# Three small transposes of the gate rows moved behind the first third of the fifth projection tile, in a one-core decoder step

## The chip, the cores and the metric

The kernel runs on one core of a Trainium2 chip. Its time is device time in microseconds (us); lower is better. TensorE (PE in the profile) multiplies, VectorE (DVE) and ScalarE (ACT) do the elementwise work, GpSimd (POOL) copies small histories, and SyncE (SP) issues the loads.

## What is computed

Two decoder layers are run on one batch of 336 tokens (256 of a prompt, 64 of eight sampled sequences, 16 meta tokens). Each layer is a half-step SwiGLU FFN, a token mixer, and a second half-step SwiGLU FFN. The part of the mixer that matters here, cut from the reference:

```
proj = h @ w_in
qkv, z = proj[..., OFF_Q:OFF_Z], proj[..., OFF_Z:OFF_BETA]
b_raw = proj[..., OFF_BETA:OFF_A]            # 4 gate columns
a_raw = proj[..., OFF_A:OFF_B]               # 4 gate columns
qkv = silu(causal_dw_conv(qkv_ext, conv_gdn))
q = l2_normalize(q of qkv) * GDN_DK ** -0.5;  k = l2_normalize(k of qkv)
beta = sigmoid(b_raw)
g = -exp(a_log) * softplus(a_raw + dt_bias)
o, s = gdn_chunks(q, k, v, beta, g, s0, chunk)
```

## The kernel before

All data is held features first: 128 features on the partitions, tokens along the row. Every float32 product of the weights is made of three passes of TensorE (L1493 to L1495, high by high, weights high by input low, weights low by input high), so each weight chunk is first split: ScalarE writes the high half (L734) and VectorE the low half (L1040). Weights come in chunks through three buffers.

The mixer's order of work is written out by hand as one list of steps, and each engine walks the same list and does its own share of each step (a step that has no share on an engine costs it nothing). So a place in the list is a place in the queue of all engines at once. The list begins with `HEAD`, and then come the parts: the projection of 28 tiles of 128 columns is cut in thirds of 3, 3 and 2 blocks of 128 features, so 9, 9 and 6 matmuls; `BEHIND_PART` says what stands behind each third. The first four tiles are made in the step `entry`, so `BEHIND_PART` begins with the first third of tile 4, the fifth tile.

The names that the prediction uses:
- `gate_rows`: TensorE multiplies the 8 gate columns (high and low) with the input, with the norm's own column sums (L1518) and row transposes (L1511, three transposes of 128x128) between.
- `gate_read`: VectorE scales the rows by the norm into ACCX (L1251).
- `gate_cols`: TensorE turns the rows into columns (L1726, three transposes); VectorE copies and adds them (L1254, L1255), adds the bias (L1259) and forms T1 (L1260), which raises `to_act`; ScalarE waits for that, then runs two exponentials (L896, L897), changes its function table, runs the logarithm (L898), and changes the table again to Silu (L899).
- `evac n`: VectorE reads projected tile n out of TensorE's output memory (L1198, L1200, L1201). `tap n`: ScalarE makes the first tap of its convolution (L838). `conv n`: VectorE makes the other three taps (L1180, three instructions). `silu n`: ScalarE (L856 to L858). `sq n`: ScalarE squares a q or k tile into SQX (L890). `sq_sum n`: TensorE sums the squares over the features (L1705).
- `gate_g`: VectorE finishes the gates (L1266 to L1273). `gb t`: TensorE spreads a column (L1662), VectorE forms the decay (L1294).
- The step `sq_sum n` waits on TensorE for `sq n`: `pe.wait_ge(qk_sq.sem, qk_sq.at(t, layer))`.

Of the kernel before, what the change touches and what calls it, by code (L numbers as in the profile page):

```python
# [105 lines left out]
def chunk_length(c):  # L106
# [3 lines left out]

FIRST_TILE = 4
HEAD = [
    ("entry",), ("gate_rows",), ("hi", 1, 0), ("evac", 0), ("tap", 0), ("hi", 1, 1), ("gate_read",), ("lo", 1, 0), ("gate_cols",),
    ("evac", 1), ("conv", 0),
]


BEHIND_PART = [
    [],
    [("evac", 2), ("evac", 3)],  # L120
    [],
    [("silu", 0), ("tap", 1), ("sq", 0), ("evac", 4), ("hi", 2, 0)],
# [1906 lines left out]
```

## Time and profile before

| | |
|---|---|
| time, median of 3 runs | 1414.47 us (1412.2 to 1415.42) |
| span of the profiled execution | 1412.4 us |
| TensorE busy | 1391.3 us, 99% of the span |
| VectorE busy | 862.0 us, 61% |
| ScalarE busy | 629.7 us, 45% |

The span runs from the first to the last instruction of one profiled execution. A time of its own outside the span is not given for that execution; the three timed runs are others. In rows of a timeline, the first number is the start and the second the time until the group's end, both in us; matmuls overlap, so the spacing of their starts (0.15 us for a matmul of 336 tokens) is what each adds.

### The profile page before, as it was taken

What the parts mean: (1) busy time and instruction counts of PE and PEld (TensorE: products, weight loads), DVE (VectorE), ACT (ScalarE), POOL (GpSimd) and SP (SyncE); (2) the same over time, 40 slices, a digit from 0 to 9 for tenths busy, and PEclk for the clock granted to TensorE, in tenths of its full rate; (3) what the DMA queues carried; (4) which work ended last, traced back from release to release, by engine and by line L of the source; (5) the groups of instructions that cost most, each with busy time, mean ns of one, the idle gap of its engine ahead of it and who ended that gap; (6) DMA issues with size and microseconds to landing.
All of it is one profiled execution on the core that took longest, in us unless ns stands there. A gap on an engine that the chain in (4) does not pass through costs nothing.

```text
span 1412.4 us, 25251 instructions
## 1 busy us (share of the span) xinstructions
PE 1391.3 (99%) x10788; PEld 1369.1 (97%) x10788; DVE 862.0 (61%) x1510; ACT 629.7 (45%) x1002; POOL 32.4 (2%) x130
## 2 busy tenths in 40 slices
PE   9999999999999999999999999999999999999997
PEld 8999999898999999999999999998999999999997
DVE  5655533787697765553376555337886968655433
ACT  5443333582644544433354333335826345444331
POOL 0000000110000000000000000001100000000000
PEclk9999999999999999999999999999999999999998
DMA  6544344422216334434435443444221263444342
GB/s 220 208 149 149 121 143 141 132 90 87 71 61 217 118 130 142 149 122 144 155 121 207 150 149 117 140 142 140 90 93 65 90 214 122 150 149 149 123 144 99
DMA packets 49760, 190.93 MB, mean 135 GB/s; under 512 B 6160, under 2 KB 8720, under 8 KB 49136
## 3 DMA queue, kind: packets, MB, share of 16 engines
q1 hardware_dynamic: 49040, 184.19, 38.9%
q0 software_dynamic: 608, 5.12, 0.9%
q8 instruction: 85, 1.39, 0.4%
q14 instruction: 27, 0.22, 0.0%
HBM read 182.86 MB, written 6.43 MB: 134 GB/s over the span
## 4 chain that ended last, share of the span: by engine, by line
PE 95%; DVE 3%; ACT 1%; issue 0%; DMA 0%; SPq 0%
PE PS L1493 27%; PE PS L1494 27%; PE PS L1495 27%; PE PS L1533 2%; PE PS L1664 2%; PE PS L1538 2%; PE PS L1534 2%; DVE WL L1040 1%; PE PS L1813 1%; PE PS L1662 1%; PE PS L1705 1%; ACT XH L751 1%; DVE XL L1052 1%; PE PS L1769 1%; PE PS L1788 1%; DVE X L1104 0%
## 5 line engine op out<-in xcount | busy, mean ns | idle before, releaser
L1493 PE MATMUL PS<-XH,WH 128*128 128x336 f32 (+1 forms) x1728 | 550.6, 319 | 0.0
L1495 PE MATMUL PS<-XH,WL 128*128 128x336 f32 (+1 forms) x1728 | 543.2, 314 | 0.0
L1494 PE MATMUL PS<-XL,WH 128*128 128x336 f32 (+1 forms) x1728 | 542.8, 314 | 0.0
L1040 DVE TENSOR_TENSOR WL<-RAW,WH 128x1024 fp32r<-128x1024 f32 (+1 forms) x312 | 398.8, 1302 | 193.3 <-ACT WH L734 192.8
L734 ACT ACTIVATE WH<-RAW 128x1024 fp32r<-128x1024 f32 (+1 forms) x312 | 343.1, 1118 | 222.0 <-DMA RAW<-in_w_down 173.3
L1493 PEld LDWEIGHTS PS<-XH,WH 128*128 128x128 f32 x1728 | 325.4, 188 | 1.4 <-issue 0.4
L1494 PEld LDWEIGHTS PS<-XL,WH 128*128 128x128 f32 x1728 | 325.5, 188 | 0.3
L1495 PEld LDWEIGHTS PS<-XH,WL 128*128 128x128 f32 x1728 | 325.2, 188 | 0.0
L1493 PE MATMUL PS<-HH,WH 128*128 128x336 f32 (+1 forms) x704 | 221.4, 314 | 0.0
L1494 PE MATMUL PS<-HL,WH 128*128 128x336 f32 (+1 forms) x704 | 221.3, 314 | 0.0
L1495 PE MATMUL PS<-HH,WL 128*128 128x336 f32 (+1 forms) x704 | 221.2, 314 | 0.0
L1146 DVE TENSOR_TENSOR GR<-PS,RB 128x336 f32<-128x336 f32 (+1 forms) x88 | 44.3, 503 | 186.5 <-PE PS L1495 186.4
L809 ACT ACTIVATE HH<-HF 128x336 fp32r<-128x336 f32 (+1 forms) x88 | 42.4, 482 | 204.3 <-DVE HF L1154 204.3
L1493 PEld LDWEIGHTS PS<-HH,WH 128*128 128x128 f32 x704 | 132.6, 188 | 0.0
L1494 PEld LDWEIGHTS PS<-HL,WH 128*128 128x128 f32 x704 | 132.2, 188 | 0.0
L1495 PEld LDWEIGHTS PS<-HH,WL 128*128 128x128 f32 x704 | 132.1, 188 | 0.0
L807 ACT ACTIVATE SG<-GR 128x336 f32<-128x336 f32 (+1 forms) x88 | 42.3, 480 | 117.8 <-DVE GR L1146 117.8
L1156 DVE TENSOR_TENSOR HL<-HF,HH 128x336 fp32r<-128x336 f32 (+1 forms) x88 | 44.4, 504 | 48.3 <-ACT HH L809 48.3
L1533 PE MATMUL PS<-XH,WH 128*128 128x336 f32 (+1 forms) x192 | 62.4, 329 | 4.6 <-DVE WL L1040 2.4
L1534 PE MATMUL PS<-XH,WL 128*128 128x336 f32 (+1 forms) x192 | 59.6, 314 | 0.0
L1538 PE MATMUL PS<-XL,WH 128*128 128x336 f32 (+1 forms) x192 | 47.6, 315 | 0.0
L1533 PEld LDWEIGHTS PS<-XH,WH 128*128 128x128 f32 x192 | 36.0, 187 | 10.7 <-DVE WL L1040 4.7
(252 smaller groups left out, 1220.7 us busy)
## 6 DMA issues: line engine op xcount, KB each, us to landing
RAW<-in_w_up SPq DMA_DIRECT2D x176, 512.0 KB, 4.3
RAW<-in_w_down SPq DMA_DIRECT2D x64, 704.0 KB, 4.1
RAW<-in_w_in SPq DMA_DIRECT2D x56, 512.0 KB, 4.3
RAW<-in_w_out SPq DMA_DIRECT2D x16, 512.0 KB, 4.2
SEQ_S<-in_states SPq DMA_DIRECT2D x2, 2048.0 KB, 9.7
out_state_s<-SEQ_S POOLq DMA_DIRECT2D x2, 2048.0 KB, 8.9
X<-in_x SPq DMA_DIRECT2D x8, 168.0 KB, 4.8
out_y<-X SPq DMA_DIRECT2D x4, 320.0 KB, 2.3
```

The source lines that it names most:

```text
L734: act.activation(WH[slot][:, cols], RAW[slot][:, cols], ACT.Copy).then_inc(split_hi.sem, 1)
L807: act.activation(SG[k][:, 0:n], GR[k][:, 0:n], ACT.Silu).then_inc(silu_done.sem, 1)
L809: act.activation(hidden(HH, c, n), HF[k][:, 0:n], ACT.Copy).then_inc(h_hi.sem, 1)
L1040: dve.tensor_tensor(WL[slot][:, cols], RAW[slot][:, cols], WH[slot][:, cols].bitcast(F32), ALU.subtract).then_inc(split_lo.sem, 1)
L1146: dve.tensor_tensor(GR[k][:, 0:n], PS[:, up_bank(c, 0), 0:n], RB[:, 0:n], ALU.mult).then_inc(gate_scaled.sem, 1)
L1156: dve.tensor_tensor(hidden(HL, c, n), HF[k][:, 0:n], hidden(HH, c, n).bitcast(F32), ALU.subtract).then_inc(h_lo.sem, 1)
L1493: pe.matmul(out, wh, xh, start=first, stop=False)
L1494: pe.matmul(out, wh, xl, start=False, stop=False)
L1495: return pe.matmul(out, wl, xh, start=False, stop=last)
L1533: pe.matmul(out, wh, XH[:, kt, 0:n], start=(kt == 0), stop=False)
L1534: pe.matmul(out, wl, XH[:, kt, 0:n], start=False, stop=False)
L1538: ins = pe.matmul(out, wh, XL[:, kt, 0:n], start=False, stop=(kt == KT - 1))
```

## The change

The step `gate_cols` leaves `HEAD`, where it stood behind `lo 1 0` and ahead of `evac 1` and `conv 0`, and stands behind the first third of tile 4.

```diff
 HEAD = [
-    ("entry",), ("gate_rows",), ("hi", 1, 0), ("evac", 0), ("tap", 0), ("hi", 1, 1), ("gate_read",), ("lo", 1, 0), ("gate_cols",),
-    ("evac", 1), ("conv", 0),
+    ("entry",), ("gate_rows",), ("hi", 1, 0), ("evac", 0), ("tap", 0), ("hi", 1, 1), ("gate_read",), ("lo", 1, 0), ("evac", 1),
+    ("conv", 0),
 ]
 BEHIND_PART = [
-    [],
+    [("gate_cols",)],
     [("evac", 2), ("evac", 3)],
```

On TensorE, at the end of `gate_rows` in the first layer, the three transposes stand ahead of tile 4 before. PS is the output memory, XH and XL the input's halves, WH and WL the weights' halves.

```order
L1714 MATMUL PS<-XH,W8X 16x336
L1726 MATMUL PS<-MK,ACCX 128x16 [waits evac_dve]
L1726 MATMUL PS<-MK,ACCX 128x16 x2
L1493 MATMUL PS<-XH,WH_59 128x336 [waits split_lo]
L1494 MATMUL PS<-XL,WH_59 128x336
L1495 MATMUL PS<-XH,WL_56 128x336
```

With the change, nine matmuls of tile 4 come first:

```order
L1714 MATMUL PS<-XH,W8X 16x336
L1493 MATMUL PS<-XH,WH_59 128x336 [waits split_lo]
L1494 MATMUL PS<-XL,WH_59 128x336
L1495 MATMUL PS<-XH,WL_56 128x336
L1493 MATMUL PS<-XH,WH_59 128x336
L1494 MATMUL PS<-XL,WH_59 128x336
L1495 MATMUL PS<-XH,WL_56 128x336
L1493 MATMUL PS<-XH,WH_59 128x336
L1494 MATMUL PS<-XL,WH_59 128x336
L1495 MATMUL PS<-XH,WL_56 128x336
L1726 MATMUL PS<-MK,ACCX 128x16 [waits evac_dve]
L1726 MATMUL PS<-MK,ACCX 128x16 x2
```

The transposes moved down by nine matmuls; nothing else moved on TensorE.

On VectorE at the same place, the four small instructions of the gate columns stand ahead of the reading of tile 1 and the convolution of tile 0 before (B_90 is the gate columns, EXT the projected tiles, CV_131 a convolution's buffer):

```order
L1251 TENSOR_TENSOR ACCX<-PS,RB 16x336 [waits filled]
L1040 TENSOR_TENSOR WL_57<-RAW_54,WH_60 128x1024 [waits split_hi]
L1254 COPY B_90<-PS 128x24 [waits small]
L1255 TENSOR_TENSOR B_90<-B_90,PS 128x24 [waits chain_dve]
L1259 TENSOR_TENSOR TOK<-B_90,GATE_P 128x12 [waits in_gate,chain_dve]
L1260 SCALAR_TENSOR_TENSOR TOK<-TOK 128x12 [waits chain_dve]
L1198 TENSOR_TENSOR EXT<-PS,RB 128x16 [waits hist_set,products]
L1200 TENSOR_TENSOR EXT<-PS,RB 128x256
L1201 TENSOR_TENSOR EXT<-PS,RB 128x8x8
L1180 SCALAR_TENSOR_TENSOR CV_131<-EXT,PAR_ALL,CV_131 128x360 [waits tap0]
L1180 SCALAR_TENSOR_TENSOR CV_131<-EXT,PAR_ALL,CV_131 128x360 [waits chain_dve] x2
```

With the change they stand behind both:

```order
L1040 TENSOR_TENSOR WL_57<-RAW_54,WH_60 128x1024 [waits split_hi]
L1198 TENSOR_TENSOR EXT<-PS,RB 128x16 [waits hist_set,products]
L1200 TENSOR_TENSOR EXT<-PS,RB 128x256
L1201 TENSOR_TENSOR EXT<-PS,RB 128x8x8
L1180 SCALAR_TENSOR_TENSOR CV_131<-EXT,PAR_ALL,CV_131 128x360 [waits tap0]
L1180 SCALAR_TENSOR_TENSOR CV_131<-EXT,PAR_ALL,CV_131 128x360 [waits chain_dve] x2
L1254 COPY B_90<-PS 128x24 [waits small]
L1255 TENSOR_TENSOR B_90<-B_90,PS 128x24 [waits chain_dve]
L1259 TENSOR_TENSOR TOK<-B_90,GATE_P 128x12 [waits in_gate,chain_dve]
L1260 SCALAR_TENSOR_TENSOR TOK<-TOK 128x12 [waits chain_dve]
L1198 TENSOR_TENSOR EXT<-PS,RB 128x16 [waits hist_set,products]
```

The four instructions passed six others. The same stands in the second layer. ScalarE's, GpSimd's and SyncE's queues keep their order.

## Rows read from the trace of the kernel before

**Rows 1.** The page: TensorE's busy time; the chain that ended last, by engine

```profile
PE 1391.3 (99%) x10788; PEld 1369.1 (97%) x10788; DVE 862.0 (61%) x1510; ACT 629.7 (45%) x1002; POOL 32.4 (2%) x130
...
PE 95%; DVE 3%; ACT 1%; issue 0%; DMA 0%; SPq 0%
```

**Rows 2.** Timeline of TensorE, first layer: start, time, engine, line, tiles, [idle before]

```profile
277.87 0.31 PE L1714 MATMUL PS<-XH,W8X 128*16 128x336 f32 x1
278.94 0.35 PE L1726 MATMUL PS<-MK,ACCX 16*128 16x16 f32 x3 [0.76 <-DVE ACCX L1251]
...
279.49 0.32 PE L1494 MATMUL PS<-XL,WH 128*128 128x336 f32 x1
```

**Rows 3.** Timeline of TensorE: three transposes in flow, between matmuls

```profile
276.63 0.31 PE L1717 MATMUL PS<-XL,W8X 128*8 128x336 f32 x1
276.78 0.49 PE L1511 MATMUL PS<-MK,RC 128*128 128x128 f32 x3
...
277.26 0.31 PE L1717 MATMUL PS<-XL,W8X 128*8 128x336 f32 x1
```

**Rows 4.** Timeline of VectorE, first layer

```profile
278.40 0.48 DVE L1251 TENSOR_TENSOR ACCX<-PS,RB 16x336 f32<-16x336 f32 x1
...
279.95 0.16 DVE L1254 COPY B<-PS 128x24 f32<-128x24 f32 x1
...
280.66 0.17 DVE L1198 TENSOR_TENSOR EXT<-PS,RB 128x16 f32<-128x16 f32 x1
...
282.96 0.17 DVE L1198 TENSOR_TENSOR EXT<-PS,RB 128x16 f32<-128x16 f32 x1
...
285.12 1.85 DVE L1180 SCALAR_TENSOR_TENSOR CV<-EXT,PAR_ALL,CV 128x360 f32<-128x360 f32 x3 [0.44 <-ACT CV L838]
```

**Rows 5.** Timeline of ScalarE, first layer: gate columns, a tap, squares

```profile
280.77 0.21 ACT L896 ACTIVATE TOK<-B 128x12 f32<-128x12 f32 x1 [0.61 <-DVE TOK L1260]
...
284.50 0.58 ACT L838 ACTIVATE CV<-EXT,PAR_ALL 128x360 f32<-128x360 f32 x1
284.99 0.51 ACT L890 ACTIVATE SQX<-QKV 128x384 f32<-128x384 f32 x1
...
288.07 0.51 ACT L890 ACTIVATE SQX<-QKV 128x384 f32<-128x384 f32 x1
...
291.59 0.51 ACT L890 ACTIVATE SQX<-QKV 128x384 f32<-128x384 f32 x1
...
312.39 0.92 ACT L890 ACTIVATE SQX<-QKV 128x384 f32<-128x384 f32 x2
```

**Rows 6.** Timeline of TensorE, first layer: the sums of squares

```profile
288.09 0.72 PE L1705 MATMUL PS<-MK,SQX 128*128 128x1 f32 x6
...
290.14 0.72 PE L1705 MATMUL PS<-MK,SQX 128*128 128x1 f32 x6
...
292.76 0.81 PE L1705 MATMUL PS<-MK,SQX 128*128 128x1 f32 x6
...
312.96 1.49 PE L1705 MATMUL PS<-MK,SQX 128*128 128x1 f32 x12
```

**Rows 7.** Timeline of VectorE, first layer: its next wait after 285.12

```profile
305.16 1.13 DVE L1294 SCALAR_TENSOR_TENSOR DA<-PS,TOK,MK 128x128 f32<-128x128 f32 x4 [0.20 <-PE PS L1662]
```

**Rows 8.** Timeline of ScalarE and TensorE, second layer: the same squares and sums

```profile
1019.38 0.92 ACT L890 ACTIVATE SQX<-QKV 128x384 f32<-128x384 f32 x2
...
1019.94 1.50 PE L1705 MATMUL PS<-MK,SQX 128*128 128x1 f32 x12
```

**Rows 9.** TensorE's two longest waits for nothing shown, first layer

```profile
340.37 0.24 PE L1788 MATMUL PS<-XM,MB 32*32 32x16 f32 x5 [0.86 <-issue]
...
350.73 0.26 PE L1769 MATMUL PS<-NB,DA 32*32 32x16 f32 x9 [1.26 <-issue]
```

**Rows 10.** Busy time and granted clock (PEclk) of the same stretch of both layers

```profile
340.00:356.00 16.00, 14.36 (x302) 13.16 (x305) 8.39 (x26) 5.51 (x12) 1.33 (x5) 0.79 0.22 69
1043.00:1059.00 16.00, 15.93 (x550) 14.64 (x550) 11.08 (x35) 8.16 (x16) 1.20 (x5) 1.00 0.22 70
```

## The prediction

> **What bounds the kernel now.** I read the page first. TensorE is busy for 99% of the span and holds 95% of the chain that ended last [rows 1]. So the time moves only when TensorE starts something earlier or later, and what counts of VectorE and ScalarE is the margin by which their results precede TensorE's need of them. Next I read TensorE's timeline around the moved step. The last matmul of the gate rows starts at 277.87, the transposes at 278.94, and the row says that TensorE sat idle for 0.76 us until VectorE had written ACCX; the second matmul of tile 4 starts at 279.49 [rows 2]. Two matmuls of tile 4 at a spacing of 0.15 would have brought that one to 278.18, so the interruption costs 1.31 us, once in each layer. Then I read the other two queues at the same place, because the step has a share in each: VectorE makes T1 from the turned columns [rows 4], and ScalarE waits for it with everything else of its queue behind [rows 5]. Last I looked for the places where TensorE needs ScalarE's results, the sums of squares [rows 6], and followed VectorE and ScalarE through both layers for idle time that could take up a delay [rows 7, 8].
>
> **What the change takes away.** Nothing is added or removed; 3 transposes, 4 VectorE instructions and the two-engine wait between them change places, twice. On TensorE, nine matmuls of tile 4 (9 x 0.15 = 1.4 us) go ahead of the transposes. The row names ACCX as the one thing that TensorE waited for there, and the weights of tile 4 were split ahead of it in VectorE's queue. They start at about 278.02 and are done at 279.40, while ACCX is written at 278.40 + 0.48 = 278.88 [rows 4], so the wait of 0.76 us should go. What three transposes in flow cost is not shown for this size. The nearest row from above is their own cost now, 279.49 - 278.94 - 0.15 = 0.40 us, with the start from standstill [rows 2]. From the other side there are three larger transposes in flow: from the matmul at 276.63 to the one at 277.26, with one more matmul between, is 0.63, of which two spacings are 0.31; so 0.32 us [rows 3]. Nothing allows less than zero. I take 0.32, the case in flow. TensorE gains 1.31 - 0.32 = 0.99 us a layer (0.91 to 1.31), 2.0 us in all, if nothing takes it back.
>
> **What the change puts later.** On VectorE the gate columns' four instructions now stand behind `evac 1` and `conv 0`. Before, the copy starts at 279.95, `evac 1` at 280.66, and the step behind `conv 0` at 282.96 [rows 4]. The two that are passed take 282.96 - 280.66 = 2.30 us, and neither waits for anything new: tile 1 was finished in `entry`, and its first tap is not needed by them. So the copy starts at 279.95 + 2.30 = 282.25, and T1 comes 2.30 us later. TensorE's columns are no bound for it: they are turned by about 279.8.
>
> ScalarE was already waiting for T1: it sat idle for 0.61 us ahead of L896 at 280.77 [rows 5]. Its queue is served in order, so L896 now starts at 283.07, and behind it come 2.30 us late: the logarithm with its two table changes, `silu 0`, `tap 1` (before at 284.50), `sq 0`, and a weight split. VectorE waits for `tap 1`: before it sat idle 0.44 us ahead of `conv 1` at 285.12, and that wait was ended by L838 [rows 4]. So `conv 1` starts at 287.42, and VectorE too is 2.30 us late with all that stands behind it, although it gained 0.7 us on `evac 1` and `conv 0`. From there both lags live on: what ScalarE waits for is VectorE's convolutions, and VectorE does not wait again until 305.16 [rows 7].
>
> **Where TensorE meets the lag.** A wait that ends lets its follower start about 0.06 us later (278.88 to 278.94 [rows 2, 4]). Now the sums of squares, each against the square that it needs [rows 5, 6]:
> - `sq_sum 0`: the square would end at 284.99 + 0.51 + 2.30 = 287.80, so TensorE starts at 287.86. It arrives at 288.09 - 0.99 = 287.10. It waits 0.76 us and stands 0.23 us ahead of before.
> - `sq_sum 1`: 288.07 + 0.51 + 2.30 + 0.06 = 290.94, before 290.14. TensorE is 0.80 us behind.
> - `sq_sum 2`: 291.59 + 0.51 + 2.30 + 0.06 = 294.46, before 292.76. TensorE is 1.70 us behind.
> - At 305.16 VectorE sat idle 0.20 us for a result of TensorE, which now comes only 1.70 us late; so this idle time takes 0.20 us of the lag, and VectorE goes on 2.10 us late [rows 7].
> - `sq_sum 6`: 312.39 + 0.51 + 2.10 + 0.06 = 315.06, before 312.96. The margin was nil, so TensorE is the full 2.10 us behind.
>
> The gain of 0.99 us is inside these figures: it only makes the first wait longer, and whether the transposes cost 0.32 or 0.40 us changes nothing. In the second layer the margin at `sq_sum 6` is nil as well: 1019.38 + 0.51 + 2.30 + 0.06 = 1022.25 against 1019.94, 2.31 us behind [rows 8]; VectorE has no idle time on the way there. Behind these points TensorE is the chain again and carries its lag to the end of the layer.
>
> The sum is 2.10 + 2.31 = 4.4 us. The span goes from 1412.4 to 1416.8. That span lies 2.1 us under the median of the timed runs and at the low end of their 3.2 us, so I add the difference to the median: 1414.47 + 4.4 = 1418.9 us, 0.31% slower. If the end of a wait cost nothing, each layer would lose 0.06 us less; a lag that is partly taken up is the second rival.
>
> **A rule that speaks against this.** TensorE is the busiest engine, with VectorE at 61% and ScalarE at 45% [rows 1], and the one gap that the change aims at is TensorE's. The Trainium skill, page "Perfetto Trace Analysis", section "Optimization Strategy", says to find the gaps on the most-contended engine and make what ends them come sooner. By the rule alone the sum would be the gap's removal, some 2 us off the time.
>
> **The rivals.**
> - The gap's removal is all that shows (0.08). TensorE keeps 0.99 us a layer, -2.0 us, 1412.5 us, not slower. For it: the idle row of 0.76 us is real, and the two late engines are idle for a third of the span or more. Against: at `sq_sum 6` the square ends at 312.90 and TensorE starts at 312.96. It decides from the point where less than 0.06 us of VectorE's 2.30 us reach that square.
> - The lag is partly taken up (0.10). If order or idle time that I have not seen absorbs it in one layer, or half in each, it is about +2.2 us, 1416.7 us. For it: at `sq_sum 2` the margin is still 0.60 us (292.76 less 292.16 [rows 5, 6]), and the rest of the loss rests on `sq_sum 6`, 20 us later, up to which every instruction of the two queues must stay in step. Against: the only idle time that I found on the way is the 0.20 us [rows 7].
> - Other stalls move (0.12). In the first layer TensorE waited 0.86 and 1.26 us for nothing that the profile shows [rows 9], and in the 16 us around it the granted clock was 0.79 of full speed, against 1.00 in the second layer [rows 10]. That is 2.1 us, and 0.21 x 16 = 3.4 us of clock: some 5.5 us that one layer has and the other has not. If they go away with another timing, the time is 1418.9 - 5.5 = 1413.4 us; if the second layer gets them too, 1424.4 us. I give 0.06 to each side. The new waits (0.8 to 1.0 us at three places in 7 us) could lower the clock too, though 0.76 us did not now.
>
> **How the numbers follow.** My forecast has 0.70, and its own range is 1416.9 to 1421.0, the spread of the runs around 4.4 us. The range of 1415.0 to 1421.5 leaves out the first rival (0.08) and the most of the third on both sides (0.11). No change within 0.2% (2.8 us) is about what a measurement of this kernel can tell. Slower by more: 0.61 of my 0.70, 0.03 of the second rival, 0.06 of the third, 0.70. Faster by more: 0.05, from the first and third. Within it: 0.25.
>
> **What would show it.** The idle time ahead of L1726 should be gone, with L1726 at about 279.4. L1254 should start at about 282.25, L896 at 283.07 after an idle time of nearly 3 us, and VectorE should wait more than 2 us for `tap 1`. TensorE should show new waits for SQX of 0.8, 1.0 and 0.9 us ahead of the first three L1705 and a fourth of some 0.4 us ahead of the seventh, and stand 2.1 us later at the last. I am wrong if L1705 shows no waits, if ScalarE runs other work ahead of L896, or if TensorE's lag shrinks behind `sq_sum 6`.

## The result, and the profile after

The change makes the kernel slower: 1424.09 us median of 6 runs (1420.97 to 1426.7) against 1414.74 us (1412.2 to 1416.45, 6 runs) for the kernel before, a ratio of 1.0072 with a 95% interval of [1.0058, 1.0086]. That is 9.4 us, where the forecast had 4.4. A second set of runs of the same kernel gave 1424.49 us (experiment 5). The profiled execution is one of the quicker ones: 1421.08 us, span 1419.3, mean granted clock 0.991.

The page of the changed kernel: TensorE's busy time, and the chain by engine.

```profile
PE 1397.0 (98%) x10788; PEld 1373.7 (97%) x10788; DVE 862.2 (61%) x1510; ACT 630.6 (44%) x1002; POOL 32.5 (2%) x130
...
PE 92%; DVE 4%; ACT 2%; issue 1%; DMA 0%; SPq 0%; ACTq 0%
```

The same 10788 matmuls now keep TensorE busy for 5.7 us more than in [rows 1], and VectorE and ScalarE have 6% of the chain instead of 4%. So there are two things to find: waits for the other two engines, and matmuls that take longer.

Timeline of VectorE, first layer, the changed kernel (columns as in [rows 4]).

```profile
280.24 0.15 DVE L1198 TENSOR_TENSOR EXT<-PS,RB 128x16 f32<-128x16 f32 x1
...
282.54 0.17 DVE L1254 COPY B<-PS 128x24 f32<-128x24 f32 x1
...
287.71 1.85 DVE L1180 SCALAR_TENSOR_TENSOR CV<-EXT,PAR_ALL,CV 128x360 f32<-128x360 f32 x3 [2.74 <-ACT CV L838]
```

Timeline of ScalarE, the same place: gate columns, the second tap, three squares.

```profile
283.37 0.21 ACT L896 ACTIVATE TOK<-B 128x12 f32<-128x12 f32 x1 [2.91 <-DVE TOK L1260]
...
287.10 0.58 ACT L838 ACTIVATE CV<-EXT,PAR_ALL 128x360 f32<-128x360 f32 x1
287.58 0.51 ACT L890 ACTIVATE SQX<-QKV 128x384 f32<-128x384 f32 x1
...
290.66 0.51 ACT L890 ACTIVATE SQX<-QKV 128x384 f32<-128x384 f32 x1
...
294.18 0.51 ACT L890 ACTIVATE SQX<-QKV 128x384 f32<-128x384 f32 x1
```

This execution is 0.29 us late from its start (the last matmul of the gate rows starts at 278.16, in [rows 2] at 277.87). Taken off, the copy L1254 is 282.54 - 279.95 - 0.29 = 2.30 us late, L896 2.31, the convolution behind the tap 2.30, and the squares 2.30, 2.30 and 2.30 [rows 4, 5]. The lag is what the prediction says, to 0.01 us, and nothing absorbs it.

Timeline of TensorE, first layer, the same kernel.

```profile
278.16 0.32 PE L1714 MATMUL PS<-XH,W8X 128*16 128x336 f32 x1
...
279.54 0.32 PE L1495 MATMUL PS<-XH,WL 128*128 128x336 f32 x1
279.78 0.35 PE L1726 MATMUL PS<-MK,ACCX 16*128 16x16 f32 x3
...
280.32 0.32 PE L1494 MATMUL PS<-XL,WH 128*128 128x336 f32 x1
...
288.14 0.83 PE L1705 MATMUL PS<-MK,SQX 128*128 128x1 f32 x6 [0.45 <-ACT SQX L890]
...
291.22 0.83 PE L1705 MATMUL PS<-MK,SQX 128*128 128x1 f32 x6 [0.76 <-ACT SQX L890]
...
292.46 0.32 PE L1493 MATMUL PS<-XH,WH 128*128 128x336 f32 x1
292.61 0.32 PE L1494 MATMUL PS<-XL,WH 128*128 128x336 f32 x1
...
294.74 1.44 PE L1705 MATMUL PS<-MK,SQX 128*128 128x1 f32 x6 [0.19 <-ACT SQX L890]
...
297.02 0.48 PE L1493 MATMUL PS<-XH,WH 128*128 128x336 f32 x1
297.31 0.48 PE L1494 MATMUL PS<-XL,WH 128*128 128x336 f32 x1
...
317.51 1.49 PE L1705 MATMUL PS<-MK,SQX 128*128 128x1 f32 x12
```

The idle time ahead of L1726 is gone. The transposes in flow cost 280.32 - 279.54 less two spacings of 0.15, 0.47 us. Three waits stand ahead of the first three sums; the idle time in their rows is 0.16 us less than the spacing lost (291.22 against 290.15 + 0.15 is 0.92, the row says 0.76). But look at the spacing of the matmuls of 336 tokens: at 292.46 it is 0.15 us, at 297.02 it is 0.29. TensorE runs at half its clock (1.2 GHz in place of 2.4) from 293.5 on, 2.3 us behind the second of these waits and ahead of the third. The second layer does the same: in the chip's record of the granted clock the stretches at half clock are 6.8 us from 293.5 and 3.4 us from 1006.9, and before the change there is none at either place.

Busy time by engine in stretches, the changed kernel (start:end, length, then PE, PEld, DVE, ACT, POOL, and behind them PEclk, DMA share, GB/s); the last row of two, then the same two of the kernel before.

```profile
279.00:325.00 46.00, 44.60 (x296) 43.51 (x295) 37.74 (x100) 34.26 (x72) 5.86 (x21) 0.93 0.24 83
986.00:1040.00 54.00, 51.89 (x388) 49.62 (x387) 46.33 (x118) 36.81 (x74) 5.96 (x21) 0.97 0.33 110
```

```profile
279.00:325.00 46.00, 46.00 (x330) 45.60 (x330) 41.83 (x108) 33.75 (x72) 5.55 (x21) 1.00 0.31 105
986.00:1040.00 54.00, 53.70 (x474) 52.88 (x475) 49.37 (x132) 33.71 (x71) 6.07 (x23) 1.00 0.29 97
```

Here is where TensorE stood at the sums of squares (starts of L1705; before from [rows 6, 8]; the 0.29 us is taken off in the first layer, and in the second the 3.75 us by which this execution enters it late, L1714 at 988.83 for 985.08):

| | before | after | later by | forecast |
|---|---|---|---|---|
| sum 0, first layer | 288.09 | 288.14 | -0.24 | -0.23 |
| sum 1 | 290.14 | 291.22 | 0.79 | 0.80 |
| sum 2 | 292.76 | 294.74 | 1.69 | 1.70 |
| sum 6 | 312.96 | 317.51 | 4.26 | 2.10 |
| sum 6, second layer | 1019.94 | 1026.97 | 3.28 | 2.31 |

Up to the third sum the forecast holds to 0.01 us. Between the third and the seventh another 2.6 us come in, of which the forecast had 0.4, and TensorE has no wait in that stretch that would explain them. The half clock also makes the other two engines later: VectorE now waits twice for TensorE, where it waited once for 0.20 us before [rows 7]. Timeline of VectorE, then ScalarE's seventh square:

```profile
303.77 1.13 DVE L1294 SCALAR_TENSOR_TENSOR DA<-PS,TOK,MK 128x128 f32<-128x128 f32 x4 [1.10 <-PE PS L1662]
...
309.71 1.13 DVE L1294 SCALAR_TENSOR_TENSOR DA<-PS,TOK,MK 128x128 f32<-128x128 f32 x4 [0.96 <-PE PS L1662]
```

```profile
316.93 0.93 ACT L890 ACTIVATE SQX<-QKV 128x384 f32<-128x384 f32 x2
```

The square starts 316.93 - 312.39 - 0.29 = 4.25 us late [rows 5], where the forecast had 2.10. So TensorE and the square come to the seventh sum together again.

### The profile page after: what moved, and what is told of

Same layout as the page of the kernel before. It is cut to its first block, busy times and chain, and to the rows that moved or that the text cites. A ratio compares the mean times of both kernels' runs of the same rounds, so it can differ in the third digit from the quotient of the medians.

```text
span 1419.3 us, 25251 instructions
## 1 busy us (share of the span) xinstructions
PE 1397.0 (98%) x10788; PEld 1373.7 (97%) x10788; DVE 862.2 (61%) x1510; ACT 630.6 (44%) x1002; POOL 32.5 (2%) x130
## 4 chain that ended last, share of the span: by engine, by line
PE 92%; DVE 4%; ACT 2%; issue 1%; DMA 0%; SPq 0%; ACTq 0%
PE PS L1493 27%; PE PS L1494 26%; PE PS L1495 26%; PE PS L1533 2%; PE PS L1664 2%; PE PS L1538 2%; PE PS L1534 2%; DVE WL L1040 1%; PE PS L1813 1%; PE PS L1662 1%; DVE CV L1180 1%; ACT XH L751 1%; DVE XL L1052 1%; PE PS L1705 1%; PE PS L1769 1%
## 5 line engine op out<-in xcount | busy, mean ns | idle before, releaser
L1493 PEld LDWEIGHTS PS<-XH,WH 128*128 128x128 f32 x1728 | 326.9, 189 | 1.5 <-issue 0.4
L1180 DVE SCALAR_TENSOR_TENSOR CV<-EXT,PAR_ALL,CV 128x360 f32<-128x360 f32 x72 | 42.5, 590 | 8.6 <-ACT CV L838 6.8
```

Source lines behind the costliest of these rows:

```text
L1180: ins = dve.scalar_tensor_tensor(cv, src[:, n, tap:tap + length - taps + 1], PAR_ALL[:, layer, col:col + 1], cv, ALU.mult, ALU.add)
L1493: pe.matmul(out, wh, xh, start=first, stop=False)
```

## The experiments

Each kernel is compared with the kernel before on the same chip. **Lost to the clock** in what follows is the span times (1 - mean granted clock), averaged over all runs of a kernel; it counts the time at half clock as the full-speed time missing in it. **Rest** is the mean time less that. The kernel before has a mean of 1414.2 us, 8.5 lost and a rest of 1405.7 on the chip of experiments 1 to 4 (23 runs); 1413.8, 8.0 and 1405.8 on that of 5 to 8 (23); 1413.9, 8.0 and 1405.9 on that of 9 to 11 (17). The edits of experiments 4, 6, 7 and 10 are shown against the change, the others against the kernel before; `gate_turn` is TensorE's share of `gate_cols`, made a step of its own.

"Lost to the clock" is no price in time by itself. Among the runs of one and the same kernel the time rises by only 0.57 to 0.85 us for each us lost, and the third wait of the change is shorter where the half clock stands ahead of it. So the difference in "lost" is the most that the clock can have cost directly, and this slope gives an estimate of what it did cost.

| kernel | median us (runs) | ratio, 95% interval | lost to the clock | rest |
|---|---|---|---|---|
| the change | 1424.09 (6) | 1.0072 [1.0058, 1.0086] | 15.9 | 1407.9 |
| 1 turns alone | 1413.46 (12) | 1.0001 [0.9988, 1.0013] | 8.6 | 1405.5 |
| 2 queues alone | 1421.94 (6) | 1.0059 [1.0043, 1.0076] | 13.7 | 1408.7 |
| 3 past one step | 1415.74 (12) | 1.0011 [1.0, 1.0023] | 9.3 | 1406.4 |
| 4 three products | 1421.78 (6) | 1.0053 [1.0038, 1.0068] | 9.9 | 1411.6 |
| 5 the change again | 1424.49 (6) | 1.0067 [1.0049, 1.0086] | 16.4 | 1407.7 |
| 6 sums later | 1422.91 (6) | 1.0059 [1.0041, 1.0077] | 17.3 | 1405.5 |
| 7 tap first | 1420.21 (12) | 1.0040 [1.0027, 1.0053] | 13.7 | 1406.1 |
| 8 turns, tap first | 1413.2 (12) | 0.9992 [0.998, 1.0004] | 8.5 | 1404.5 |
| 9 sums early | 1423.73 (6) | 1.0068 [1.0051, 1.0085] | 15.2 | 1408.0 |
| 10 one product | 1421.21 (6) | 1.0048 [1.0035, 1.006] | 11.6 | 1409.5 |
| 11 as 8, split later | 1411.63 (12) | 0.9982 [0.997, 0.9994] | 7.4 | 1404.0 |

**1. TensorE's share alone.** The transposes move, VectorE's and ScalarE's gate columns stay.

```diff
-    [],
+    [("gate_turn",)],
...
-                    elif what == "gate_cols":
+                    elif what == "gate_turn":
```

> TensorE's share of the step (the three transposes) moves behind the first third of tile 4; VectorE's and ScalarE's shares stay where they were before. Theory one, the loss is VectorE's and ScalarE's lag and what follows from it: no lag, so TensorE keeps the 0.99 us a layer up to the sums of squares, where the margin is nil, so it gives most back: between 0 and 2.0 us faster than before, ratio 0.9986 to 1.0000, no wait ahead of the first three L1705. Theory two, the loss comes from the transposes' new place in TensorE's queue or another timing of its code: slower, up to the 9 us of the change, ratio up to 1.007.

No change that can be told. The early sums have no wait in the first layer, and the gain is kept up to the sixth sum: it starts at 310.50, the seventh at 312.93. Timeline of TensorE, this kernel, at the sixth and seventh sum.

```profile
310.50 0.72 PE L1705 MATMUL PS<-MK,SQX 128*128 128x1 f32 x6
...
312.93 1.50 PE L1705 MATMUL PS<-MK,SQX 128*128 128x1 f32 x12 [0.22 <-ACT SQX L890]
```

There it waits for the square, and stands where it stood before, at 312.96 [rows 6]. This execution reaches the place 0.20 us later (L1714 at 278.07 for 277.87), so 0.23 us of the gain are kept at the seventh sum of the first layer; in the second it starts at 1023.21 with L1714 at 988.35, and nothing is kept. What the transposes give is paid back at the sum that had no margin. The ratio lies 0.0001 above the forecast's range of 0.9986 to 1.0000.

**2. The other two queues alone.** The transposes stay (as `gate_turn`), the gate columns of VectorE and ScalarE move as in the change.

```diff
-    ("gate_cols",),
-    ("evac", 1), ("conv", 0),
+    ("gate_turn",), ("evac", 1), ("conv", 0),
...
-    [],
+    [("gate_cols",)],
```

> The opposite half: TensorE's transposes stay at their place of before, VectorE's and ScalarE's shares move as in the change. Theory one: the same final lag of TensorE as in the change, 2.1 and 2.3 us in the two layers, so 4.4 us of waits; the first wait of 0.76 us for SQX is gone, because TensorE arrives 1 us later, and the second and third stay near 0.8 and 0.9 us. With the clock falling as in the change: ratio 1.006 to 1.007; without it 1.003. Theory two: ratio 1.000.

This alone costs 1422.4 - 1414.2 = 8.2 us by the means. Its waits, from the timeline of TensorE:

```profile
290.66 0.83 PE L1705 MATMUL PS<-MK,SQX 128*128 128x1 f32 x6 [0.64 <-ACT SQX L890]
...
294.17 1.44 PE L1705 MATMUL PS<-MK,SQX 128*128 128x1 f32 x6 [0.39 <-ACT SQX L890]
...
1002.73 0.83 PE L1705 MATMUL PS<-MK,SQX 128*128 128x1 f32 x6 [0.76 <-ACT SQX L890]
1006.25 1.16 PE L1705 MATMUL PS<-MK,SQX 128*128 128x1 f32 x6 [0.67 <-ACT SQX L890]
```

The loss comes with the late queues. There are 6.8 us of half clock from 293.2 and as much from 1006.6. The first begins ahead of the second wait of its layer, so a single new wait of 0.64 us went before it.

**3. Past one step instead of two.** The whole step goes behind `evac 1` and stays ahead of `conv 0`.

```diff
-    ("gate_cols",),
-    ("evac", 1), ("conv", 0),
+    ("evac", 1),
+    ("gate_cols",), ("conv", 0),
```

> A smaller dose: the whole step moves past evac 1 alone, so VectorE's lag is 0.54 us in place of 2.30, and TensorE's queue is that of before. Theory one: nothing at the first three sums (their margins were 2.5, 1.5 and 0.6 us); at the seventh 0.3 us behind in the first layer and 0.5 in the second, so 0.9 us in all, ratio 1.0006, and a full clock from 286 to 312 us. If the lag carried a cost of its own that does not go by margins, a quarter of the change's loss: 2.2 us, ratio 1.0016.

The seventh sum is the only one that meets the lag, and no half clock is granted in either early stretch: PEclk is 1.00 in 279 to 325 and in 986 to 1040. Timeline of TensorE, the seventh sum:

```profile
313.35 1.50 PE L1705 MATMUL PS<-MK,SQX 128*128 128x1 f32 x12 [0.17 <-ACT SQX L890]
```

0.39 us later than in [rows 6], and 0.32 with this execution's late start taken off (L1714 at 277.94); in the second layer the seventh sum is at 1019.89 with L1714 at 984.50 for 985.08, 0.53 us late. The forecast had 0.3 and 0.5. The time is 1.5 us longer by the means, with an interval from 1.0 to 1.0023, so the times alone don't tell the 0.9 us of the margins from the 2.2 us of the other theory; the places in the trace do.

**4. Work in the waits.** The change, and TensorE multiplies three throwaway products of 128 columns ahead of its wait at the first three sums (the profile shows them as six matmuls of 0.83 us together). They go to free banks of its output memory and nobody reads them.

```diff
+                        if t < 3:
+                            if t == 2:
+                                pe.wait_ge(proj_read.sem, proj_read.at(4, layer))
+                            for _ in range(3):
+                                pe.matmul(PS[:, 7 if t == 2 else 6, 0:P], mask("ident"), mask("ident"), start=True, stop=True)
                         pe.wait_ge(qk_sq.sem, qk_sq.at(t, layer))
```

> The change, and in the new waits TensorE runs three throwaway products of 128 columns (about 0.75 us) ahead of each of the first three waits for SQX in each layer. They write nothing that is read. Theory one with the clock's fall caused by these waits: TensorE has no standstill worth its name there, the clock stays at full speed from 286 to 312 us and at the same place of the second layer, and only the lag of 4.4 us is left, or up to 1 us more where the products outlast a wait: ratio 1.003 to 1.004. If the clock falls whatever TensorE does there: ratio 1.006 to 1.008.

At the place itself it does what it is meant to. Busy time in stretches, this kernel, and its seventh sums in both layers:

```profile
279.00:325.00 46.00, 45.70 (x329) 44.88 (x328) 39.68 (x105) 33.95 (x72) 5.86 (x21) 1.00 0.27 90
986.00:1040.00 54.00, 53.29 (x473) 52.16 (x472) 47.07 (x129) 32.74 (x70) 4.72 (x22) 1.00 0.26 86
```

```profile
315.36 1.50 PE L1710 MATMUL PS<-MK,SQX 128*128 128x1 f32 x12 [0.21 <-ACT SQX L890]
...
1020.86 1.50 PE L1710 MATMUL PS<-MK,SQX 128*128 128x1 f32 x12 [0.42 <-ACT SQX L890]
```

Full clock in both, and the first seventh sum is 315.36 - 312.96 = 2.40 us later, less 0.31 us of this execution's late start 2.09. The second is 0.92 us later, and L1714 is 1.38 us early there (983.70), so 2.30. The forecast has 2.10 and 2.31, and waits at both places: with the clock held, its count of the lag is right in both layers. Over before on the same chip, lost to the clock is 1.4 us in place of the change's 8.4 (experiment 5), but the rest is 5.9 us more in place of 1.9, so the time is still 7.3 us over before, against 10.3. The forecast for the time, a ratio of 1.003 to 1.004, was missed, and the intervals of this kernel and of the change overlap. In the profiled execution part of the loss shows later, in bursts of small matmuls:

```profile
342.91 0.37 PE L1793 MATMUL PS<-XM,MB 32*32 32x16 f32 x23 [1.14 <-issue]
350.76 0.42 PE L1774 MATMUL PS<-NB,DA 32*32 32x16 f32 x27 [0.27 <-issue]
...
1048.92 0.39 PE L1793 MATMUL PS<-XM,MB 32*32 32x16 f32 x10 [1.45 <-issue]
```

The kernel before has no such wait at the third place, and here 10.2 us of half clock begin in it, at 1048.2. What these waits are, and why added instructions move them, stays open.

**5. The change again**, with no edit, on the chip of experiments 6 to 8.

> The change itself once more, beside the next three on one chip, for the clock of each run. Theory one (waits of 4.4 us, and the clock's fall behind the crowded waits on top): every run has a lower mean clock than the runs of before beside it, by 0.004 to 0.006, and ratio 1.006 to 1.008. Theory three (the time lost beyond the waits is a chance fall of the clock elsewhere): the clock of the two kernels overlaps and the ratio comes down toward 1.003.

1424.49 us; by the means 10.3 us over before, of which at most 8.4 are the clock's. By the slope above these 8.4 us are 4.8 to 7.1 us of time, an estimate, and leave 3.2 to 5.5 us for the waits; the forecast's 4.4 lies in that. This pair is what the other kernels are held against. Its waits are 0.43, 0.74 and 0.62 us, and 0.50, 0.83 and 0.66, and the half clock follows both groups, at 296.5 and at 1009.9.

**6. The first three sums one third later.** The change, with `sq_sum` 0, 1 and 2 moved down so that TensorE meets the late squares later.

```diff
-    [("gate_g",), ("silu", 1), ("sq_sum", 0), ("tap", 3)],
-    [("sq", 1), ("conv", 2), ("sq_sum", 1), ("lo", 1, 1), ...
+    [("gate_g",), ("silu", 1), ("tap", 3)],
+    [("sq", 1), ("conv", 2), ("sq_sum", 0), ("lo", 1, 1), ...
...
-    [("silu", 3), ("tap", 5), ("silu", 4), ("cum",), ("sq_sum", 2), ("lo", 2, 1), ("sq", 3), ("evac", 6)],
-    [("conv", 5)],
+    [("silu", 3), ("tap", 5), ("silu", 4), ("cum",), ("sq_sum", 1), ("lo", 2, 1), ("sq", 3), ("evac", 6)],
+    [("conv", 5), ("sq_sum", 2)],
```

> The change, with the first three sums of squares each one third of a tile later in the list of steps, so that TensorE does real matmuls in the time in which it waited. The lag of VectorE and ScalarE stays. Theory one: no waits for SQX up to 294 us; the lag is met in smaller waits, at the starts of tiles 7 and 8 (about 0.7 us each) and at the seventh sum (about 1 us), so the same 4.4 us of lag, but the clock stays up at 294 us: ratio 1.003. If the crowded early waits were the whole loss: ratio 1.000. If the clock falls whatever TensorE does: 1.006 or more.

The waits for squares are gone, and another takes their place: TensorE now reaches a weight chunk ahead of its low half, which the late VectorE makes. Timeline of TensorE, and its busy time in the stretch:

```profile
293.19 0.39 PE L1493 MATMUL PS<-XH,WH 128*128 128x336 f32 x1 [1.05 <-DVE WL L1040]
```

```profile
279.00:325.00 46.00, 44.95 (x303) 44.49 (x302) 38.50 (x101) 33.93 (x72) 5.64 (x21) 0.93 0.24 84
```

One wait of 1.05 us was followed by half clock too, 1.6 us later. In the second layer 10.2 us of half clock begin at 1001.4, inside a wait of 1.04 us that ends at 1002.02. So it isn't needed that several waits stand close together. The forecast for this kernel, full clock and 1.003, was missed, and the wait on WL wasn't in it; so the experiment doesn't show what the clock does without new waits. Lost to the clock are 9.2 us more than before at a time 9.0 us longer: most of this loss is the clock's, but by the slope not all of it need be.

**7. The change with the second tap first.** ScalarE makes `tap 1` ahead of its wait for the gate columns, so VectorE doesn't wait for it.

```diff
-    ("conv", 0),
+    ("tap", 1), ("conv", 0),
...
-    [("silu", 0), ("tap", 1), ("sq", 0), ("evac", 4), ("hi", 2, 0)],
+    [("silu", 0), ("sq", 0), ("evac", 4), ("hi", 2, 0)],
```

> The change, with tap 1 put ahead of the gate columns, so that ScalarE does it while it waits for T1 and VectorE does not wait 2.7 us for it. Theory one says that this wait carries the lag from ScalarE to VectorE: VectorE's lag at the third convolution falls from 2.3 to about 1.1 us, TensorE's at the seventh sum to about 1.1 and 1.3 us, 2.4 us in all for the two layers, and the early waits become 0.5, 0.9 and 0.3 us: ratio 1.002 with a full clock, up to 1.004 with a falling one. If the lag has another path, no better than the change: 1.0065.

4.3 us quicker than the change by the means of the same chip: the passage from ScalarE back to VectorE through `tap 1` carried part of the lag. Waits of 0.58 us at 290.3 and 0.64 us at 998.8 remain, and the half clock with them, 6.8 us from 292.9 and 10.2 us from 999.5. In the first layer the wait of 0.58 us is the only one of TensorE ahead of it.

**8. Turns alone, and the second tap first.** Experiment 1 with the move of `tap 1` from experiment 7.

```diff
-    ("evac", 1), ("conv", 0),
+    ("evac", 1), ("tap", 1), ("conv", 0),
...
-    [],
+    [("gate_turn",)],
```

> TensorE's three transposes behind the first third of tile 4, VectorE's and ScalarE's shares as before, and tap 1 ahead of silu 0 on ScalarE, so that VectorE's wait of 0.44 us for it goes. Theory one: the margins at the first three sums rise, and at the seventh sum the lead is some 0.4 us plus what the first layer's nil margin allows: the times of the trace of before, carried through, give 1.0 us less in all, ratio 0.9993. If only TensorE's own work sets the time, 2 us less, 0.9986; if a new order costs, above 1.000.

0.8 us less than before by the means, within the interval. At the seventh sum TensorE stands at 312.88 and 1019.46. Against L1714 of the same layer (278.53 and 984.02) that is 0.74 us ahead of before in the first layer and 0.58 us behind in the second. That second layer has 3.4 us of half clock from 998.5 with no wait of TensorE in the profile there, PEclk 0.97 in 986 to 1040: the one fall in these stretches that no wait goes ahead of.

**9. Waits without the change.** This is the kernel before, its gate columns where they were, with the second and third sum brought forward so that TensorE reaches them too early.

```diff
-    [("gate_g",), ("silu", 1), ("sq_sum", 0), ("tap", 3)],
-    [("sq", 1), ("conv", 2), ("sq_sum", 1), ("lo", 1, 1), ...
-     ("lo", 2, 0), ("conv", 4), ("hi", 3, 1), ("evac", 5)],
-    [("silu", 3), ("tap", 5), ("silu", 4), ("cum",), ("sq_sum", 2), ("lo", 2, 1), ...
+    [("gate_g",), ("silu", 1), ("sq_sum", 0), ("tap", 3), ("sq_sum", 1)],
+    [("sq", 1), ("conv", 2), ("lo", 1, 1), ...
+     ("lo", 2, 0), ("conv", 4), ("hi", 3, 1), ("sq_sum", 2), ("evac", 5)],
+    [("silu", 3), ("tap", 5), ("silu", 4), ("cum",), ("lo", 2, 1), ...
```

> Here VectorE, ScalarE and the gate columns stay as before the change; only TensorE's second and third sums of squares stand one third of a tile earlier or a little more, so that TensorE reaches them before their squares are ready. Before, the squares end at 288.58 and 292.10 us and TensorE starts the sums at 290.14 and 292.76, so the waits should be some 0.6 and 0.9 us in the first layer and as much in the second; TensorE ends up 1.5 us late in each layer, and by the waits alone the kernel is 2.9 us slower (about 1417). Theory A (new waits in this crowded stretch bring TensorE's clock down, whatever caused them): half clock behind the waits in one or both layers, and several us more than the waits, 1419 to 1422 us. Rival B (the clock falls for another reason that goes with the late gate columns): full clock there in both layers as before, and 1417 us.

1423.73 us: about the change's loss, without its late queues, and more than either theory had. The first two sums ran together without a wait, so there is one new wait in each layer and not two. Timeline of TensorE, then its busy time in stretches:

```profile
290.44 0.32 PE L1495 MATMUL PS<-XH,WL 128*128 128x336 f32 x1
291.93 1.44 PE L1705 MATMUL PS<-MK,SQX 128*128 128x1 f32 x6 [1.18 <-ACT SQX L890]
293.23 0.63 PE L1493 MATMUL PS<-XH,WH 128*128 128x336 f32 x1
293.66 0.48 PE L1494 MATMUL PS<-XL,WH 128*128 128x336 f32 x1
293.94 0.48 PE L1495 MATMUL PS<-XH,WL 128*128 128x336 f32 x1
...
1003.33 0.83 PE L1705 MATMUL PS<-MK,SQX 128*128 128x1 f32 x6 [1.26 <-ACT SQX L890]
```

```profile
279.00:325.00 46.00, 44.82 (x288) 44.38 (x287) 36.06 (x95) 33.81 (x71) 5.33 (x21) 0.89 0.25 84
986.00:1040.00 54.00, 51.85 (x351) 50.06 (x349) 45.20 (x114) 36.92 (x74) 5.92 (x21) 0.94 0.31 105
```

The matmul before the wait is at full speed, those behind it at half; in the second layer the half clock begins 2.0 us behind the wait, at 1005.3. Lost to the clock is 7.2 us more than before, the rest 2.1 us more; the change has 8.4 and 1.9 (experiment 5). The two waits are 1.18 + 1.26 = 2.4 us of the 9.3 us by which the means differ. So new idle time of TensorE in this stretch is followed by the half clock without anything of VectorE's lag. The edit also puts the small matmuls of two sums side by side, and whether that has a part was not tried.

**10. One product instead of three.** As experiment 4, with `range(1)`.

> The change with one throwaway product of 128 columns in place of three ahead of each of the first three sums. The waits shrink by the time of one product each, some 0.06 us, and stay 0.4 to 0.7 us. If the length of the waits in the crowded stretch decides about the clock, one product is too little, the half clock comes back in both layers, and the time is that of the change, 1422 to 1424 us. If it is what stands ahead of the wait (any product directly ahead of it), full clock at 279 to 325 us and 1419 us.

Full clock does not come back. Timeline of TensorE and the first stretch:

```profile
288.05 0.83 PE L1710 MATMUL PS<-MK,SQX 128*128 128x1 f32 x6 [0.21 <-ACT SQX L890]
...
291.12 0.83 PE L1710 MATMUL PS<-MK,SQX 128*128 128x1 f32 x6 [0.53 <-ACT SQX L890]
```

```profile
279.00:325.00 46.00, 45.26 (x302) 44.40 (x301) 37.66 (x100) 34.16 (x72) 5.75 (x21) 0.93 0.23 81
```

The half clock begins at 293.6 and 1007.0, 6.8 us long each. So a product directly ahead of the wait is not enough; that the remaining idle time (0.53 and 0.60 us at most) is what counts fits, but isn't shown apart. Over all runs 3.6 us more than before are lost to the clock, between experiment 4's 1.4 and the change's 8.4, and the time of 1421.21 us lies just under the forecast's 1422 to 1424.

**11. The margin at the seventh sum opened.** Experiment 8, and ScalarE's high half of one weight chunk, 0.95 us, goes behind squares 6 and 7. This was tried to see whether the nil margin is what keeps the gain of the transposes from showing.

```diff
-    [("conv", 8), ("sq_sum", 4), ("silu", 6), ("hi", 4, 1)],
+    [("conv", 8), ("sq_sum", 4), ("silu", 6)],
...
-    [... ("sq", 6), ("sq", 7), ("sq_sum", 6), ("sq_sum", 7), ...
+    [... ("sq", 6), ("sq", 7), ("hi", 4, 1), ("sq_sum", 6), ("sq_sum", 7), ...
```

> TensorE's share alone moved, the second tap ahead, and in addition one weight split of ScalarE (high half, 0.95 us) behind the squares 6 and 7 instead of ahead of the seventh tile's Silu. The seventh square should then end nearly 1 us earlier, at about 311.4 us, so that TensorE keeps there what the transposes in flow gave it (1.0 us less what the earlier waits take). If the nil margin at the seventh sum is what took the gain back, TensorE stands 0.6 to 1.0 us ahead behind the seventh sum in each layer, and the kernel is 1.5 us faster than before, about 0.1%. Rival: the split is late for TensorE's use of it, or the gain is taken back at a later wait; then 0 to 1 us slower.

1411.63 us, 0.9982 [0.997, 0.9994]: quicker than the kernel before, and than the change by 12 us. ScalarE's timeline, then TensorE's:

```profile
310.60 0.93 ACT L890 ACTIVATE SQX<-QKV 128x384 f32<-128x384 f32 x2
311.43 2.94 ACT L734 ACTIVATE WH<-RAW 128x1024 fp32r<-128x1024 f32 x3
```

```profile
312.01 1.39 PE L1705 MATMUL PS<-MK,SQX 128*128 128x1 f32 x12
```

The squares start at 310.60 for 312.39 in [rows 5], and TensorE passes the seventh sum 0.95 us ahead of [rows 6], without a wait. Against L1714 of the same layer it is 0.83 us ahead in the first (277.75 for 277.87) and 1.01 in the second (1014.22 and 980.37). So the gain of the transposes is kept once the margin is there. By the means, the rest is 1.9 us less than before and the clock 0.6.

## Why the prediction was wrong in size

- **The gain of the transposes.** 0.99 us a layer was forecast, inside the first wait. The transposes in flow cost 0.47 us and not 0.32, outside the two bounds that the prediction had for them (0.32 and 0.40), so the gain is 0.84. It changes nothing in the sum, as the prediction says: it makes the first wait 0.15 us shorter. That this gain can't be kept at the seventh sum is shown by experiments 1 and 11. With it the first rival's condition was wrong too: experiment 1 has no lag at all at that square and keeps 0.23 and 0.00 us, not 0.99 in each layer.
- **The lag of VectorE and ScalarE.** 2.30 us forecast, 2.30 measured, through the path named (T1, the gate columns, the second tap, the second convolution).
- **TensorE's place at the first three sums.** -0.23, 0.80 and 1.70 forecast, -0.24, 0.79 and 1.69 measured.
- **The seventh sum.** 2.10 and 2.31 us forecast, 4.26 and 3.28 measured, 3.1 us more in all. Here the sum fails. In the change TensorE doesn't wait there, since both it and the square come that late. With full clock (experiment 4) it does wait there, and is 2.09 and 2.30 us late, so the lag was counted rightly and something was added to it.
- **The term that was wrong: the clock at nothing.** The sum of 4.4 us has every matmul outside the waits at its old duration. The prediction names the clock only in the rival "other stalls move", by the words "The new waits (0.8 to 1.0 us at three places in 7 us) could lower the clock too, though 0.76 us did not now", and gives it no price and no more than 0.06. It measured 6.8 us at half clock in the first layer and 3.4 in the second of the profiled execution, so 5.1 us of full-speed time, and 3.1 us of that are seen at the seventh sums; over all runs 8.4 us are lost, some 4.8 to 7.1 us of the 10.3 by which the means differ (experiment 5). The lost time and the waits don't simply add, since time at half clock ahead of a wait shortens the wait: the third wait is 0.19 us in the profile of the change and 0.62 in that of experiment 5.
- **The inference behind it.** That 0.76 us ahead of L1726 did not lower the clock was read as a sign that these waits would not. But the length of a wait does not decide alone. One new wait of 0.58 us (experiment 7), 0.64 (2), 1.05 (6) or 1.18 us (9) stood ahead of the half clock in the first layer, while the kernel before keeps full clock behind waits of 1.40 and 0.97 us of TensorE that end at 8.39 and 11.47 us. In the early stretch the waits stand among small matmuls (L1705 with one column, L1732 to L1736 with 4 to 36), ahead of L1726 among full ones. Which part the small matmuls have was not tried by itself and stays open.
- **A sign in its own rows.** In the kernel before, the half clock stands at 340.9 and 351.2, 3.4 us each, and each begins 0.5 us behind one of the two waits of [rows 9], among matmuls of 16 columns. The prediction took the waits and the clock of [rows 10] as one thing that might go away or double, and didn't ask whether the one brings the other. Experiment 11 has waits of 0.86 and 0.73 us at these places and full clock, so it isn't certain each time.
- **A reading without effect.** The span of 1412.4 us was held to be at the low end of the timed runs. In the runs of the change and the experiments the time is some 1.8 us more than the span, so this execution lies near their median, where the forecast put it anyway.
- **The rival from the Trainium skill**, the page "Perfetto Trace Analysis", section "Optimization Strategy", is refuted as a forecast for the change: the gap named went away and 9.4 us came.

TensorE's clock, then, was to be asked about wherever the change adds waits. In every kernel here with a new wait of more than 0.5 us in this stretch the half clock began at the latest 2.6 us behind the last of them (the change twice, experiments 2, 6, 7, 9, 10). With waits of up to 0.22 us in the first layer and 0.42 in the second it did not (1, 3, 4, 11, and the first layer of 8); the second layer of experiment 8, above, shows that a wait isn't its only cause. The Trainium skill, page "TensorE: Matmul & The Clock Gate", section "A second HAM failure mode: psum-queue depth-cycling", tells of a kernel in which TensorE idles briefly and often between groups of matmuls and its clock swings between both levels; the traces here agree in part, with a few single waits of 0.58 to 1.26 us in place of many small ones.

What stays open: why the clock's share of the first layer's later stretch (some 340 to 355 us) differs from run to run of one and the same kernel (3.4 us of half clock in one profile of the change, 10.2 in the other), what brings 3.4 us more of it at 385.7 and 388.7 in both profiles of the change alone, and what the 4 us are by which experiment 4's rest is longer than the change's.

## What to carry to other kernels

Before a step is moved to close a gap on the busiest engine, follow its shares on the other engines to the next place where the busiest engine needs them, and to the place with the smallest margin; a gain shows only if it passes that one. If the move adds idle time of half a microsecond or more to a TensorE that was full, price the clock too: here it cost an estimated 5 to 7 us, about as much as the waits or more. Move the shares of a step separately where the list allows it: TensorE's alone, with the margin opened, gave a kernel 0.18% quicker, while all together gave one 0.72% slower.

## What the runs showed of the hardware

- Among small matmuls, TensorE's granted clock fell to its lower level behind single idle times of 0.58 us (experiment 7), 0.64 (2), 1.05 (6) and 1.18 us (9), and behind groups of 0.4 to 0.8 us. Three throwaway products ahead of each wait kept it at full speed there, one did not.
- The idle time of 0.76 us ahead of L1726 is followed by no fall in the kernel before, in either layer, nor are the 1.40 and 0.97 us that end at 8.39 and 11.47 us.
- While TensorE ran at half clock, VectorE waited 1.10 and 0.96 us for its results, against 0.20 us before, and so the square that TensorE needs next came later as well.
- The times of one kernel's runs go with the clock: over the kernels here the time rises by 0.57 to 0.85 us for each us lost to it, and the kernel before ranges from 1411.6 to 1418.0 us that way.
- Three transposes of 16 columns in flow between matmuls of 336 cost 0.47 us, more than from standstill (0.40) and more than three of 128 columns (0.32).
